# Two transformer blocks on one core: modulation rows spread over twelve groups, compression's matrices loaded ahead, and compressed scores that wait for fewer things

## The reference, cut to what matters

```
mod = silu(c) @ ada_w + ada_b                   # 6 x 2048: 96 columns of 128
h   = rmsnorm(x) * (1 + sc1) + sh1
z   = h @ w_in    # split into q, kc, vc, ks, vs, kw, vw, gates, lx, ly, ga, gb
k_cmp, v_cmp = gelu(blocks(kc) . w1_k) @ w2_k, the same for vc   # 15 blocks of 32 tokens
o_a = g0 * attend(q, k_cmp, v_cmp) + g1 * attend(q, ks, vs) + g2 * attend(q, kw, vw)
o_b = gelu(ly) * rg_lru(conv(lx))
x   = x + g1 * (sigmoid(ga) * (o_a @ proj_a) + sigmoid(gb) * (o_b @ proj_b)) @ w_out
x   = x + g2 * conv_glu_ffn(rmsnorm(x) * (1 + sc2) + sh2)
```

## Time and profile before

| | us |
|---|---|
| median of 3 runs | 2901.43 (2900.73 to 2903.86) |
| profiled execution | 2896.86 |
| its span in the trace | 2895.1 |
| TensorE busy | 2662.9 (92%) |
| VectorE busy | 1864.0 (64%) |
| ScalarE busy | 1090.7 (38%) |
| GpSimd busy | 201.0 (7%) |

### The profile page before, as it was taken

One profiled execution on the slowest core, in us unless ns is written; L12 is line 12 of the kernel. 1 busy time (PEld: TensorE's weight loads), 2 busy tenths in 40 slices (PEclk: granted clock), 3 DMA queues, 4 the chain that ended last, 5 costly groups with the idle time before them and its releaser, 6 DMA issues.

```text
span 2895.1 us, 47700 instructions
## 1 busy us (share of the span) xinstructions
PE 2662.9 (92%) x20334; PEld 2562.5 (89%) x20334; DVE 1864.0 (64%) x2583; ACT 1090.7 (38%) x1350; POOL 201.0 (7%) x172
## 2 busy tenths in 40 slices
PE   6979787997999999899999999999898888889999
PEld 4778776997899999799999999999888777789999
DVE  6854555666576666578975566654558777777563
ACT  1022342553433333335443344444333443434432
POOL 0000000000000000000265520000000000000000
PEclk9978897999999999899999999999999898999999
DMA  8946352442677777377766665555464433345554
GB/s 352 425 173 213 121 196 95 160 139 95 226 271 281 277 263 255 123 276 262 242 217 208 220 214 181 188 178 171 134 204 147 131 120 125 126 157 170 176 192 145
DMA packets 237251, 568.08 MB, mean 196 GB/s; under 512 B 11216, under 2 KB 15312, under 8 KB 222576
## 3 DMA queue, kind: packets, MB, share of 16 engines
q1 hardware_dynamic: 227568, 530.31, 53.2%
q0 software_dynamic: 9472, 34.74, 3.2%
HBM read 550.85 MB, written 14.16 MB: 195 GB/s over the span
## 4 chain that ended last, share of the span: by engine, by line
PE 70%; DVE 13%; DVEq 5%; ACT 4%; DMA 4%; issue 2%; PEld 0%; PEldq 0%; SPq 0%; POOL 0%; ACTq 0%
PE pair L1622 60%; DVE wlo L1129 4%; DMA wraw<-w_in_dram 2%; PE pair L1201 2%; ACT whi L1124 2%; PE bank L1201 1%; PE bank L1206 1%; PE bank L409 1%; DVE wraw L1105 1%; DMA wraw<-ffn_up_dram 1%; DVEq L1021 1%; DVEq L321 1%; DVEq L847 1%; PE pair L1628 1%; PE bank L609 1%
## 5 line engine op out<-in xcount | busy, mean ns | idle before, releaser
L1129 DVE TENSOR_TENSOR wlo<-wraw,whi 128x1024 fp32r<-128x1024 f32 x777 | 964.2, 1254 | 851.2 <-ACT whi L1124 829.4
L1124 ACT ACTIVATE whi<-wraw 128x1024 fp32r<-128x1024 f32 x777 | 809.1, 1056 | 1555.8 <-PE pair L1622 927.2
L1622 PE MATMUL pair<-h_hi,whi 128*128 128x256 f32 x3936 | 1146.2, 291 | 24.8 <-DVE h_lo L331 15.6
L1622 PE MATMUL pair<-h_lo,whi 128*128 128x256 f32 x3936 | 1129.8, 287 | 0.0
L1622 PE MATMUL pair<-h_hi,wlo 128*128 128x256 f32 x3936 | 1128.6, 287 | 0.0
L1622 PEld LDWEIGHTS pair<-h_hi,whi 128*128 128x128 f32 x3936 | 773.2, 196 | 48.0 <-issue 39.8
L1622 PEld LDWEIGHTS pair<-h_lo,whi 128*128 128x128 f32 x3936 | 773.0, 196 | 0.7
L1622 PEld LDWEIGHTS pair<-h_hi,wlo 128*128 128x128 f32 x3936 | 771.8, 196 | 0.0
L1105 DVE SCALAR_TENSOR_TENSOR wraw<-wraw,cb 128x2048 f32<-128x2048 f32 x96 | 218.8, 2286 | 18.6 <-DMA wraw<-ada_wT_dram 17.9
L1622 PE MATMUL pair<-hid_hi,whi 128*128 128x256 f32 x768 | 218.5, 284 | 0.0
L1622 PE MATMUL pair<-hid_lo,whi 128*128 128x256 f32 x768 | 217.3, 283 | 0.0
(11 more groups left out here) (416 smaller groups left out, 3321.8 us busy)
## 6 DMA issues: line engine op xcount, KB each, us to landing
wraw<-w_in_dram SPq DMA_DIRECT2D x156, 1024.0 KB, 5.2
wraw<-ada_wT_dram SPq DMA_DIRECT2D x96, 1024.0 KB, 5.4
wraw<-ffn_up_dram SPq DMA_DIRECT2D x96, 1024.0 KB, 5.1
wraw<-ffn_down_dram SPq DMA_DIRECT2D x48, 1024.0 KB, 5.1
wraw<-w_out_dram SPq DMA_DIRECT2D x32, 1024.0 KB, 5.1
wfour<-w_in_dram SPq DMA_DIRECT2D x16, 1024.0 KB, 9.3
wraw<-proj_a_dram SPq DMA_DIRECT2D x16, 1024.0 KB, 7.1
wraw<-proj_b_dram SPq DMA_DIRECT2D x16, 1024.0 KB, 6.1
```

The lines of the kernel that those rows point to most:

```text
L1124: sc.activation(whi[:, r, 0:w], wraw[:, z % RAW, 1024 * half:1024 * half + w], ACT.Copy).then_inc(hi_ready, 1)
L1129: ve.tensor_tensor(wlo[:, z % RAW, half, 0:w], wraw[:, z % RAW, 1024 * half:1024 * half + w], whi[:, r, 0:w].bitcast(F32), ALU.subtract).t ...
L1622: ins = te.matmul(pair[:, o, :], w[:, at_w + o * P:at_w + (o + 1) * P], x, start=(k == 0 and o % 2 == 0 and t == 0), stop=(k == last and t ...
```

## The change

Five things change. (1) Rows 32 to 47: k1 and v1 keep two each; the other twelve stand one per group, behind slot 1 of q0 to q3, lx0 to lx3 and ly0 to ly3. (2) `wcmp` and `w2` get a second buffer and a semaphore for each; POOL loads the keys' matrices in the prologue when 30 rows are done, and the values' when TensorE has finished the prologue's last matmul and VectorE its last split; `compress` only keeps a bare `yield` where its hand-over to POOL was. (3) In the prologue kc and vc are evicted ahead of the split of unit 3 (and of the row that goes with it). (4) In nsa(1) to nsa(3) TensorE waits for the eviction of q(i) and for ScalarE's reading of lru(i-1)'s gates, not for VectorE's drain. (5) With that hand-over its `yield` goes too, so these three jobs have 26 steps; nsa(0) keeps 27.

```diff
-    at = [(out[of(kind, i)], s) for kind, i in (("k", 1), ("v", 1), ("q", 0), ("q", 1), ("lx", 0), ("ly", 0), ("q", 2), ("lx", 1))
-          for s in (1, 3)]
+    at = [(out[of(kind, 1)], s) for kind in ("k", "v") for s in (1, 3)]
+    at += [(out[of("q", i)], 1) for i in range(4)] + [(out[of(kind, i)], 1) for i in range(4) for kind in ("lx", "ly")]
+    at.sort(key=lambda a: (out.index(a[0]), a[1]))
     for n, (g, s) in enumerate(at):
         g.ada[s] = [32 + n]
...
-    w2 = put("w2", z2 + 29 * K + 256, [P, P])
+    w2 = [put("w2_k", z2 + 29 * K + 256, [P, P]), put("w2_v", z2 + 28 * K + 512, [P, P])]
...
-    wcmp = put("wcmp", z1, [P, 32, P])
+    wcmp = [put(f"wcmp{n}", z1 + 16 * n * K, [P, 32, P]) for n in range(2)]
...
-        yield from j.hand("to_pool", "dve", "pool", j.drained())
-        if me == "pool":
-            if which == 1:
-                j.eng.wait_ge(S["pe_to_dve"], j.ready["cmp"][0])
-            po.dma_start(wcmp[:, :, :], small["cmp_w1"][which].rearrange("l d e -> d l e")).then_inc(wcmp_in, 16)
-            po.dma_start(w2[:, :], small["cmp_w2"][which]).then_inc(wcmp_in, 16)
+        yield
...
-            j.eng.wait_ge(wcmp_in, 32 * (which + 1))
+            j.eng.wait_ge(wcmp_in[which], 32)
...
-        yield from j.hand("to_pe", "dve", "pe", j.drained())
+        if i == 0:
+            yield from j.hand("to_pe", "dve", "pe", j.drained())
+        elif me == "pe":
+
+            j.eng.wait_ge(*evacuated("q", i))
+            j.eng.wait_ge(S["act_to_dve"], j.ready["gates read"][i - 1])
...
                 li_made = j.give("act_to_dve", "act", ins)
+                j.ready["gates read"].append(li_made)
...
-        for u in range(U4, U4 + 4):
+        if me == "pool":
+
+            for which in range(2):
+                if which == 0:
+                    j.eng.wait_ge(ada_done, 2 * DC - 2)
+                else:
+                    j.eng.wait_ge(pe_units, U4)
+                    j.eng.wait_ge(S["to_pe"], j.ready["h1"][-1])
+                po.dma_start(wcmp[which][:, :, :], small["cmp_w1"][which].rearrange("l d e -> d l e")).then_inc(wcmp_in[which], 16)
+                po.dma_start(w2[which][:, :], small["cmp_w2"][which]).then_inc(wcmp_in[which], 16)
+        for u in range(U4, U4 + 3):
             split_unit(j, u)
         for g in range(2):
             for _ in evac(j, g):
                 pass
+        split_unit(j, U4 + 3)
         split_unit(j, U4 + 4)
```

## The result

The changed kernel takes 2823.28 us (median of 4 runs, 2822.49 to 2825.24), the kernel before 2902.64 (2900.73 to 2904.44). The ratio is 0.9728, 95% interval 0.9711 to 0.9745: 79 us less. The two profiled executions are 2896.86 and 2822.66 us, so the traces show 74 us of the gain.

A forecast was written before the change was run, and what follows sets the result against it. It took TensorE's waits behind late weight transfers, crowded by two rows per group, as the bound. Terms -19 - 26 - 4 - 2 + 3 + 1.6 - 7 - 3.8 + 0 = -57 gave 2844 us, range 2818 to 2880.

The forecast's parts named there:

- The rows: One row per group takes weight transfers off TensorE's path: nsa(0) -19 us, nsa(1) -26, lru(0) -4, q0 -2.
- The late rows' price: Rows moved to later groups: 1 us each in lru(1) to lru(3), +3 in all; 2.3 us each in nsa(2) and nsa(3).
- The upper price of a row: Upper bound for a moved row, from what one cost before in nsa(1): (99.80 - 71.00)/4 = 7.2 us.
- The scores' wait: Start of nsa(1) to nsa(3): L445's stall mostly moves to L485; 2 us gained in nsa(1), nsa(2) +1.6, nsa(3) -7, rows included.
- Compression: Wait at L409 in k1: weight load without the matrices beside it takes 4.9 us, so -3.8 us (0 to -6).
- Prologue: Earlier eviction wins 3.3 us, early matrices cost up to 5.1 us of transfer; taken as 0, from -5 to +11.
- The +1.8 for even sharing: Prologue, if SP's and POOL's queues share evenly: SP's loads up to 5.1 us later, over the 3.3 won.
- One row still binding: Rival: with one row per group, transfers still bind; nsa(0), nsa(1) and the stretch between keep half their excess; 2871 us, chance 0.18.
- Cost by the row: Rival: each moved row costs later the 7.2 us it gave, and the prologue loses 11; 2909 us, chance 0.05.
- The step count's edit giving nothing: Rival: schedule edit gains nothing, as L485's same-unit wait eats it and nsa(3)'s alignment doesn't help; 2858 us, chance 0.12.
- Nothing moving at all: Rival: the drain is replaced by waits equally long; 2901 us, chance 0.03.
- The signs: Trace marks named beforehand as showing the forecast right or wrong: ScalarE's idle times, job lengths, clock, L445, L485, L409, first L1622.

The follow-up runs named there:

- small_rows: Kernel before, rows 36 to 47 keeping their ring places and VectorE work but loading 16 KB of their 1 MB each: 2901.70 us, ratio 0.9987.
- no_place: Kernel before, rows 36 to 47 without ring place or load, VectorE's work for them kept: 2844.52 us, ratio 0.9797.
- rows_only: Kernel before with the modulation rows spread as in the change, and nothing else: 2836.66 us, ratio 0.9772.
- late_matrices: Changed kernel, but POOL issues the keys' matrices after the prologue's last matmul and the values' after six units of k1: 2816.41 us, ratio 0.9696.
- rows_late: Kernel before with rows 36 to 47 two per group in the late groups (ly1, q3, lx2, ly2, lx3, ly3): 2921.37 us, ratio 1.0057.
- keep_27: Changed kernel with the removed yield put back, so nsa(1) to nsa(3) keep 27 steps: 2825.06 us, ratio 0.9730.
- wait_only: Kernel before with only the scores' wait changed and 26 steps in nsa(1) to nsa(3): 2875.50 us, ratio 0.9907.
- lead_4: Kernel before with splits four units ahead of TensorE instead of five: 2822.74 us, ratio 0.9722.
- best: late_matrices with the removed yield put back in nsa(1) and nsa(2) alone: 2807.05 us, ratio 0.9664.

## Why the prediction was right, and where its terms were off

**The rows: mechanism right, size too small.** The ring's distance was the cause (small_rows, no_place), and one row per group did let the transfer out of TensorE's path, but for 1.6 us in nsa(0). The term mis-sized is nsa(0): 19 forecast with 22 as its bound, 28.3 measured. I had built it from nsa(2)'s 71.0 us, which itself holds 3.4 us of waiting at L445 and a clock of 0.93. A job without long waits runs at clock 1.00 and in 67.7. A reference stage must be cleared of its own stalls before it serves as a floor. nsa(1): 26 forecast, 24.1 measured, and that is in part luck: the rows alone gave 27.5 (rows_only), the wait 1.8 more, and the step count, priced at nothing, took 5.1 back. lru(0): 4 against 6.9, outside the bound of 5.5; the bound was its idle time alone, and its clock rose too, from 0.96 to 1.00. The late rows' price in the lru windows was 0, not 3: TensorE is busy all the time in lru(1) and lru(2), so the row is hidden there, and lru(3) gets no further row (five before and after, with pa0). In nsa(2) and (3) the rows cost 3.4 and 4.0, against 4.6 and 2.3. The upper price of a row, 7.2 us, was 28.8 us shared by four rows, but VectorE computes three in nsa(1) before, so it is 9.6; no term of the sum used it.

**The scores' wait.** "The rest of the stall only moves to the transposes" was right: L445 to nothing, 22.4 us at L486. The three waits are 9.4, 7.7 and 5.3 us instead of "2 to 5"; with the step put back they are 5.3, 4.2 and 7.6. nsa(2) +0.9 against +1.6. nsa(3), -11.6 against -7: the step count gave 9.4 where I had 6. The fault is nsa(1) and (2): I named that two steps would meet in one unit and that rows fall on it, and still priced the step count at nothing there. It cost 5.1 and 2.9 us.

**Compression.** L409's wait went from 13.5 to 9.8, as forecast (9.7). But late_matrices has the same wait with the keys' load issued at 148.10 instead of 134.17. What had to go was the neighbour of one transfer: the weights ahead of L405 take 4.86 us there (from 159.69), 8.71 before. The load need not stand in the prologue for that.

**Prologue.** Taken as 0, it was +2.9. Both sides of that term came out larger: the earlier eviction is worth 4 to 5 us where I had 3.3, and the matrices cost 6 to 8 (155.72 against 147.91; 154.7 against 148.5 by the means) where I had at most 5.1. The +1.8 for even sharing was the better guess, but the sharing was not even in bytes. The packets in the trace of the changed kernel show it: from 140 to 147 us POOL's queue has 449 packets of 4 KB, 263 GB/s, and SP's 452, nearly all of 2 KB, 133 GB/s. The load of the first k1 weights, issued by SP at 128.72, ahead of POOL's at 134.17, landed at 149.66; before, issued at 129.20, at 143.37. The Trainium skill's rule (DMA: Bandwidth & Descriptors, "Queues, rings and completion order"), that an engine alternates between queues packet by packet, agrees with the trace: 449 packets against 452. The load at 166 us that the forecast named for it was issued behind POOL's, so it shows sharing, not that an earlier load is slowed.

**Rivals.** One row still binding, at half the excess: no, nsa(0) has no wait of TensorE over 1.7 us. Cost by the row: rows_late shows 34 and 48 us in nsa(2) and (3) for two rows per group, where one per group costs 3 to 4. The step count's edit giving nothing: true in sum for the count (keep_27), not for the wait, which gives 13 us. Nothing moving at all: no.

**The signs.** Those that came true: the clock above 0.9, nsa(1) in 72 to 80 us, no wait at L445 in nsa(1) to (3), L409's wait. Those that missed: ScalarE's waits for w_in reached 4.4 us in nsa(0) and 3.8 in nsa(1), not under 3; nsa(0) took 67.7, less than 72; the first L1622 came at 155.72, not by 155; the waits at L485 were longer. One sign of being wrong was set badly: nsa(2) longer than before (71.9 against 71.0) was forecast by the sum itself.

**The sum by trace.** +2.9 start, -2.5 k1, -1.2 v1 and gates, -1.2 q0, -28.3, -6.9, -24.1, 0, +0.9, 0, -11.6, -2.8 in lru(3) and pa0, +0.7 behind: -74. The -2.8 was not forecast. wait_only and lead_4 show it too, rows_only, keep_27 and best do not; I can't say what decides it. Why the rest of some kernels is up to 4 us off stays open as well.

## What to carry to other kernels

Where a ring of loads is shared by two kinds of tenants, count for each slot how many units lie between its release and its use; each tenant shortens that distance by its place, whatever its bytes, and evenly spread it may cost next to nothing. Where hand-over steps are queued behind prefetched work on the same engine, less lead can be faster than more (0.9722 here, by one constant): each split taken early stands ahead of the small steps. And a load "as early as possible" can cost more than it gives if the DMA engines are full then: issue it at the first moment with room that still precedes its use.

## What the runs showed of the hardware

TensorE's pauses cost twice. In nsa(0) 21 us of idle time (95.95 less 74.71) came with a granted clock of 0.86 and 74.7 us of busy time; with 2 us of idle time the clock is 1.00 and the same 506 matmuls take 65.6. So 28 us came back for 19 us of idle time removed, nearly half as much again. In compression the 64 small matmuls for the keys take 13.9 us at a granted clock of 0.50, after 9.8 us of waiting as after 13.5; the 64 for the values, with no wait ahead of them, take 7.09 us at 1.00. So the shorter wait gave back none of that. The windows of the kernel before, keys and values:

```profile
185.32:199.23 13.91, 13.91 (x65) 13.91 (x66) 3.44 (x3) 0.00 (x0) 0.00 (x0) 0.50 0.00 0
255.79:262.88 7.09, 7.09 (x66) 7.09 (x65) 2.30 (x2) 0.00 (x0) 0.00 (x0) 1.00 0.18 75
```

In the one stretch where this was counted, two queues with work shared the DMA engines by packets (as the profile counts them), not by bytes: 449 packets of 4 KB against 452 nearly all of 2 KB in 7 us of the changed kernel's prologue, 263 against 133 GB/s. So the load in small packets was the one that lost most.
